# A decoder block with expert retrieval on one core: the front in five batches (1, 1, 2, 2, 2 chunks) instead of four (1, 2, 3, 2)

## What is computed

```python
x = x + mixed @ w_out
xn = rmsnorm(x, ffn_norm_g)
q = xn @ wq
v1, i1 = top_k(s1, 16); v2, i2 = top_k(s2, 16)
best, pos = top_k(v1[..., :, None] + v2[..., None, :], 16)
idx = i1 * 128 + i2 at pos; g = softmax(best)
act = gelu(einsum('td,thkd->thk', xn, u_tab[idx]))
y = einsum('thk,thkd->td', g * act, v_tab[idx])
out = rmsnorm(x + y, final_norm_g)
```

## Time and profile before

| | |
|---|---|
| median of 3 runs | 3487.49 us |
| the profiled execution, its own time | 3493.22 us |
| its span, first to last instruction | 3491.5 us |
| mean granted clock of TensorE | 0.849 |
| busy: PE / DVE / ACT / POOL | 2454.5 / 2663.4 / 687.7 / 1382.3 us |
| weight tiles loaded | 96 + 32 + 64 = 192 of 512 KB |
| front of chunk 0, until the first gathers' product | 133.4 us |
| chunk 0, up to its final sum | 556.8 us |
| chunks 1, 2 | 452.2, 446.5 us |
| chunks 3, 4, 5 | 384.4, 392.9, 392.8 us |
| chunks 6, 7 | 362.1, 360.5 us |

### The profile page before, as it was taken

One profiled execution on the slowest core, in us unless ns is written; L12 is line 12 of the kernel. 1 busy time (PEld: TensorE's weight loads), 2 busy tenths in 40 slices (PEclk: granted clock), 3 DMA queues, 4 the chain that ended last, 5 costly groups with the idle time before them and its releaser, 6 DMA issues.

```text
span 3491.5 us, 29071 instructions
## 1 busy us (share of the span) xinstructions
PE 2454.5 (70%) x7552; PEld 1321.4 (38%) x7552; DVE 2663.4 (76%) x6520; ACT 687.7 (20%) x1947; POOL 1382.3 (40%) x1296
## 2 busy tenths in 40 slices
PE   8569895589989785675878787576667555554554
PEld 7447463246545342223544333243223222211221
DVE  1674689865778799897779788689877577777776
ACT  2122311121434111112114332111111111111111
POOL 0132323333334333444445445344444344444442
PEclk9779998899999897887889899898788777777777
DMA  6878697789888998889999999999888899999997
GB/s 217 313 299 325 266 381 292 292 334 356 331 330 329 380 355 311 325 339 368 415 411 377 341 370 388 387 394 371 334 356 340 337 374 380 380 370 372 380 383 293
DMA packets 185037, 1212.83 MB, mean 347 GB/s; under 512 B 20672, under 2 KB 20672, under 8 KB 53440
## 3 DMA queue, kind: packets, MB, share of 16 engines
q0 software_dynamic: 147456, 1073.81, 78.7%
q1 hardware_dynamic: 37440, 137.40, 10.4%
HBM read 1198.54 MB, written 12.58 MB: 347 GB/s over the span
## 4 chain that ended last, share of the span: by engine, by line
PE 34%; DVE 29%; DMA 23%; ACT 6%; issue 5%; POOL 2%; POOLq 0%; DVEq 0%; ACTq 0%; SPq 0%
DMA ring<-in_uv,cur_idx 22%; PE vacc L900 17%; DVE ring L1075 11%; PE bank L938 6%; DVE acc L1106 4%; ACT diag L731 3%; PE bank L1006 3%; PE o_ps L904 2%; POOL ring L694 2%; DMA xn<-in_final_norm_g 1%; PE bank L934 1%; DVE lt L1223 1%; DVE ocT L1233 1%; PE bank L949 1%; PE bank L967 1%
## 5 line engine op out<-in xcount | busy, mean ns | idle before, releaser
L900 PE MATMUL vacc<-ring,diag 128*128 128x512 f32 x2048 | 1267.1, 763 | 985.5 <-ACT diag L731 983.2
L694 POOL DMA_INDIRECT ring<-in_uv,cur_idx x1024 | 1215.1, 1187 | 1172.5 <-PE vacc L900 611.6
L1075 DVE CUSTOM_DVE_ANT_0 ring<-ring,xn 128x1024 f32<-128x1024 f32 x1024 | 1219.5, 1222 | 351.6 <-DMA ring<-in_uv,cur_idx 349.0
L900 PEld LDWEIGHTS vacc<-ring,diag 128*128 128x128 f32 x2048 | 481.7, 246 | 1670.2 <-ACT diag L731 1027.2
L1106 DVE SCALAR_TENSOR_TENSOR acc<-ring,g_w,acc 128x512 f32<-128x512 f32 x832 | 625.6, 752 | 35.2 <-DVE g_w L1098 0.6
L685 POOL COPY cur_idx<-idx 128x4 uint32<-128x4 uint32 (+1 forms) x256 | 165.2, 645 | 904.9 <-DVE acc L1106 693.6
L726 ACT ACTIVATE g_ex<-g_cu 128x4 f32<-128x4 f32 x256 | 52.4, 205 | 2071.6 <-DVE g_cu L1088 2055.3
L731 ACT ACTIVATE diag<-ident,g_w 128x128 f32<-128x128 f32 x1024 | 326.8, 390 | 187.8 <-DVE g_w L1098 184.5
L938 PE MATMUL bank<-hT,wpool 128*128 128x256 f32 (+2 forms) x1280 | 285.0, 382 | 1.4 <-ACT hT L757 1.4
L938 PEld LDWEIGHTS bank<-hT,wpool 128*128 128x128 f32 x1280 | 219.8, 192 | 69.1 <-issue 12.1
L1017 PE MATMUL bank<-hT,wpool 128*128 128x256 f32 (+2 forms) x1024 | 235.9, 386 | 0.7 <-ACT hT L839 0.7
(11 more groups left out here) (126 smaller groups left out, 1798.2 us busy)
## 6 DMA issues: line engine op xcount, KB each, us to landing
wpool<-in_w_in SPq DMA_DIRECT2D x96, 512.0 KB
wpool<-in_peer_wq SPq DMA_DIRECT2D x64, 512.0 KB
wpool<-in_w_out SPq DMA_DIRECT2D x32, 512.0 KB
ring<-in_uv,cur_idx POOLq DMA_INDIRECT x1024
xb<-in_x SPq DMA_DIRECT2D x15, 512.0 KB
x_scratch<-xb SPq DMA_DIRECT2D x8, 512.0 KB
xn_scratch<-xb SPq DMA_DIRECT2D x8, 512.0 KB
xn<-xn_scratch SPq DMA_DIRECT2D x8, 512.0 KB
```

The costliest lines, as they stand in the source:

```text
L694: nc.gpsimd.indirect_dma_start(ring[:, s, :], None, uv, bass.IndirectOffsetOnAxis(ap=cur_idx[:, s:s + 1], axis=0))\
L900: ins = nc.tensor.matmul(vacc[:, :], diag[:, q, s, :], ring[:, q * GROUP + s, D:D + PE_COLS], start=first and s == 0, stop=last and s == G ...
L1075: ins = nc.vector.tensor_tensor_reduce(out=ring[:, s, 0:D], in0=ring[:, s, 0:D], in1=xn[:, c % 2, :], scale=1.0, scalar=0.0, op0=ALU.mult, ...
```

## The change

Five batches stand in the table in place of four: [0], [1], [2, 3], [4, 5], [6, 7]. Batch 1 is chunk 1 alone and runs under chunk 0; [2, 3] under chunk 1; [4, 5] under chunks 2 and 3; [6, 7] under chunks 4 and 5. The widest batch has 256 tokens instead of 384, so `hT`, `qT` and `ocT` shrink by a third. `KEYS_STAY` becomes 3, since values of chunks 4 and up are first stored by batch 3 now; there are two loads of the keys as before. `COST_T` keeps the planner's costs on 384 tokens. `wide_groups` follows the order: 8, 17 and 23 groups in chunks 0, 2 and 5 before, 7, 8, 16 and 15 in chunks 0, 1, 3 and 5 now.

```diff
-BATCHES = [[0], [1, 2], [3, 4, 5], [6, 7]]
+BATCHES = [[0], [1], [2, 3], [4, 5], [6, 7]]
...
-KEYS_STAY = 2
+KEYS_STAY = 3
...
+COST_T = 3 * P
...
-            scale = len(BATCHES[bi]) * P / TMAX if name in BY_TOKENS else 1.0
+            scale = len(BATCHES[bi]) * P / COST_T if name in BY_TOKENS else 1.0
```

## The result

The median is 3535.51 us (3527.85 to 3537.61, 4 runs) against 3489.8 us (4 runs of the kernel before); the ratio is 1.012 with a 95% interval of 1.0092 to 1.0149, that is 42 us slower, with an interval of 32 to 52. The forecast was 3509 us, slower by 22, in a range up to 3552: the sign and the range held, and the forecast change was half of the measured one. The profiled execution's span is 3532.8 us, 41 more than before. (PE is TensorE, DVE VectorE, ACT ScalarE, POOL GpSimd, SP SyncE.)

What follows compares the result with a forecast made beforehand. Gathers were taken as the base load, with front work holding them up in dense stretches. Batch excesses 75 + 156 + 105 + 95 = 431 against 409 gave +22 us on 3487.5, so 3509 us, range 3450 to 3552.

Steps and rivals of the forecast that it cites:

- The yardstick: Chunks 6 and 7 carry no front: 11.3 us a group; what a stretch takes beyond that is its excess.
- Weights are not simply added: The fifth reading's 25.2 MB need 61 us of all DMA engines, but lie under gathers, partly in stretches below full rate.
- Batch 2 at 156: Chunks 2 and 3, prepared in chunk 1: excess 156 us (projections 37, attention 48, query 30, search 41), ends 140 and 180.
- Batch 1 at 75: Chunk 1, prepared in chunk 0: excess 75 us (projections 26, attention 12, query 25, search 12), ends 39 and 110.
- Rival 2: Chunk 0 nearly free: its excess falls to 50, later batches near their lower ends, 3456 us; chance 0.27.
- Batch 3 at 105: Chunks 4 and 5, prepared in chunks 2 and 3: excess 105 us, including 10 for a wait; ends 82 and 125.
- Batch 4 at 95: Chunks 6 and 7, prepared in chunks 4 and 5: excess 95 us (projections 19, attention 32, query 18, search 26), ends 82 and 120.
- The stall: DVE's 18.4 us wait for the final gain at chunk 2's start moves to chunk 3's start; 10 us counted.
- Rival 3: Late SP work: gain or a chunk's rows come late at a second start, another 10 to 18 us, 3525 us; chance 0.08.
- Rival 1: Every byte is paid: 25.2 MB more weights cost 61 us whole, better balance gives nothing, 3549 us; chance 0.15.
- The rule of the Trainium skill: HBM binds at about 358 GB/s a core, so the fifth reading costs an estimated 70 us, in all some 3558 us.

Runs made afterwards that it cites:

- Thin weights: Changed kernel with 48 weight tiles of one batch cut to an eighth: batch 1 3493.27, batch 2 3525.51, batch 4 3502.27 us; kernel before, its batch 3: 3464.73 us.
- The fewer-blocks runs: Chunks 6 and 7 attend only to their own and the first three key blocks, 14 of 30 left out: changed kernel 3490.82 us, kernel before 3477.44 us.
- the run with more groups: Changed kernel with the planner's costs of attention times 1.5, so batch 4's 30 blocks lie under 27 groups instead of 23: 3508.87 us.
- the one with four readings: Kernel with batches [0], [1, 2], [3, 4], [5, 6, 7], against the kernel before: 3539.36 us, ratio 1.015.
- the one with five: Kernel with batches [0], [1, 2], [3, 4], [5, 6], [7], against the kernel before: 3505.76 us, ratio 1.0053.

## Why the prediction was right, and where its size was off

- **The yardstick and the method** held: the excess by phases adds up to the difference of the spans, 43 of 41 us. Chunk 0 is faster by 88 us and chunk 1 slower by 73, where I had said 80 and 60.
- **Weights are not simply added:** right. Thin weights gave 35, 4 and 23 us by batch in place of 54.
- **Batch 2 at 156:** 154, phase by phase within 6 us (36, 50, 24, 44 for 37, 48, 30, 41), and PE's whole stretch was the right bound of its projections.
- **Batch 1 at 75:** 76, with some luck: the projections cost 18 where I had 26 and the search 19 where I had 12. That bytes bound it is borne out in part: thin weights took 32 of its 76 us. Rival 2 (chunk 0 nearly free) fails on its first term, 76 where it needed 50.
- **Batch 3 at 105:** 98, and that is luck too. Attention came out at 42 and not 31; as cut here the query has 10 groups where I counted 12, and the search 19 where I counted 17, so those two are better read together, 34 against 55. Errors of +11 and -21 partly cancel there.
- **Batch 4 at 95:** 125. This is the term that was mis-sized: "attention, 30 blocks in 23 groups at 12.7 us, 32". It took 13.7 us a group, 56. I had put it between the paces of batch 2 and batch 3 before, 13.55 and 11.96, as if the first bounded it from above; it was no upper end. And 12.7 lay low even between them: a straight line by blocks a group (1.5 and 0.83, here 1.3) gives 13.1, an excess of 41. So some 9 of the 24 us were my choice within the two rows, and 15 lay beyond them. Search, with 16 planned groups instead of 23, cost 34 where I took 26. The fewer-blocks runs and the run with more groups both put the loss in this place.
- **The stall:** one of 18.4 before and one of 14.9 us after, at the start of chunk 3 as the order showed. Ten us for it was too much: in the kernel before, five such waits of 44.3 us together are worth 8. Rival 3 (a second wait above 10 us ahead of chunk 6) didn't appear: the changed kernel has one.
- **Rival 1** (every byte paid): its 3549 us lies nearer to the measured 3535.5 than my 3509, and it is still wrong as a mechanism for the whole. Its own sign, stages of batches 1 and 2 with a DMA share above 0.95, appeared in three of batch 1's four stages (1.01, 0.98, 0.96) and in one of batch 2's (0.96; the others 0.94, 0.75, 0.74). Chunk 0 is also where thin weights gave most, 35 of 54 us. In the other three cases they gave less than half of its price, and of the kernels with other batches the one with four readings costs more than the one with five.
- **The rule of the Trainium skill** ("DMA: Bandwidth & Descriptors", section Bandwidth: about 358 GB/s a core between HBM and SBUF) would have given an estimated 3558 us. Here the trace disagrees again: 412, 416 and 415 GB/s in three projection stretches. The same section gives this figure as a core's share when both cores of an HBM domain stream, while this program runs on one core.

## What to carry to other kernels

Measure what side work costs as the excess of each stretch over a stretch without it, and price a move by the density that the work meets afterwards. Two stretches of a kernel are not a scale for a third: its price can lie beyond both, and the same blocks were cheaper or dearer by 14 us with another order. Say how a value between two rows was chosen. Before blaming bytes, thin them out in one place: where PE was busy for the whole stretch, the same bytes were free.

## What the runs showed that I had not expected

The output projection frees eight weight slots at once, so SP sends eight tiles of 512 KB within 4 us. Between 2403 and 2428 us of the changed kernel the DMA queues moved (packets, MB, share of the engines):

```profile
q0 software_dynamic: 670, 4.96, 48.0%
q1 hardware_dynamic: 1223, 4.49, 46.6%
```

The gathers (queue 0) got about half of the engines, 4.96 MB in 25 us, while such a burst drained; alone they move 4.2 MB in 11.3 us. The group that waited for them took 21 us, with DVE waiting 2.5 to 3.0 us ahead of each of its four dot products. The kernel before has the same burst in its batch 3 (eight tiles sent from 2199 to 2203 us, a group of 21 us), so it is no part of what made batch 4's attention dearer. Here the burst halved the rate of the gathers beside it. Spreading it over the next groups was not tried.

The waits of DVE for the gain were worth far less than their length (a fifth in the kernel before), and a change of the planner's costs that gave 22 us in one kernel took about 14 in another that differs by its batches.
